# A hybrid decoder step on one core: shift rows moved ahead in the sync queue, past forget rows loaded early, pass-one units two to a tile, sample keys turned in pairs

## What is computed

```
h = x @ w_in                                   # columns for four head groups
A  y_a = u * (w_s @ LN(v) + b_s)               # u, v = gelu of two column ranges
B  s = q k^T/8 + c[q] - c[k]; p = softmax(s); y_b = p v      # "fox": c = cumsum(log forget)
C  gates * (compressed, selected, window attention)          # "nsa": one kv head per branch
   k_cmp = gelu(blocks of 32 rows @ w1) @ w2
D  y_d = d_b * conv3(d_c * d_h)
   samples: the same with keys and values taken from paged caches
x = LN(alpha*x + concat(y_a..y_d) @ w_out);  x = LN(alpha*x + MoE(x))
out: y, new k/v rows, log forget rows, window state, conv state (last 2 rows of d_c*d_h), v of A
```

## Time and profile before

| | us |
|---|---|
| median of 3 runs | 1379.12 (1375.01 to 1380.24) |
| the profiled execution | 1370.15 |
| its span, first to last instruction | 1368.4 |
| PE busy | 1162.9 (85%) |
| DVE busy | 419.5 (31%) |
| ACT busy | 316.4 (23%) |
| mean granted clock of PE, of full speed | 0.898 |

### The profile page before, as it was taken

The page is one execution under the profiler, slowest core; times in us unless marked ns, Lnnn a source line. Parts: engine busy times, 40 slices in busy tenths (PEclk is TensorE's granted clock), DMA queues, the critical chain, the costliest instruction groups (busy, mean ns, idle before and its releaser), DMA issues.

```text
span 1368.4 us, 13724 instructions
## 1 busy us (share of the span) xinstructions
PE 1162.9 (85%) x4624; PEld 609.5 (45%) x4625; DVE 419.5 (31%) x908; ACT 316.4 (23%) x628; POOL 82.3 (6%) x124
## 2 busy tenths in 40 slices
PE   7999998899999864998679989999389999999800
PEld 6647654344545321335444534555244444444400
DVE  2112433354435311114232312324611111111158
ACT  0102334452211531432211101111011111111133
POOL 3100000000000010000000000000011101011062
PEclk9999999999998886997659999998589999999965
DMA  7201103101000920300600614112258776957373
GB/s 224 80 20 54 62 0 122 28 2 45 1 1 2 21 46 19 108 1 0 184 1 9 240 62 154 62 62 78 92 177 293 279 248 231 321 193 277 143 290 132
DMA packets 105034, 149.23 MB, mean 109 GB/s; under 512 B 23482, under 2 KB 78074, under 8 KB 104954
## 3 DMA queue, kind: packets, MB, share of 16 engines
q1 hardware_dynamic: 88250, 112.63, 27.8%
q0 software_dynamic: 6464, 22.56, 4.7%
q10 hardware_dynamic: 10272, 13.40, 2.7%
HBM read 118.50 MB, written 32.02 MB: 110 GB/s over the span
## 4 chain that ended last, share of the span: by engine, by line
PE 77%; DVE 9%; SPq 5%; DMA 4%; issue 3%; ACT 2%; POOL 0%; POOLq 0%; DVEq 0%; ACTq 0%
PE psum_all L1305 17%; PE psum_all L1863 12%; PE psum_all L1783 9%; PE psum_all L1421 7%; PE psum_all L1851 6%; PE psum_all L1376 4%; PE psum_all L1451 3%; DMA arena<-in_w_exp_down 3%; PE psum_all L1485 2%; SPq L799 2%; PE psum_all L1834 1%; PE psum_all L1517 1%; PE psum_all L1538 1%; PE psum_all L1693 1%; PE psum_all L1600 1%
## 5 line engine op out<-in xcount | busy, mean ns | idle before, releaser
L1305 PE MATMUL psum_all<-arena 128*128 128x512 f32 (+7 forms) x800 | 236.8, 468 | 0.0
L1863 PE MATMUL psum_all<-arena 128*128 x400 | 181.8, 609 | 11.9 <-DMA arena<-in_w_exp_down 9.7
L1305 PEld LDWEIGHTS psum_all<-arena 128*128 128x128 f32 (+1 forms) x800 | 131.3, 183 | 91.4 <-issue 65.7
L1863 PEld LDWEIGHTS psum_all<-arena 128*128 128x128 f32 x400 | 76.1, 195 | 100.4 <-issue 100.4
L1783 PE MATMUL psum_all<-arena 128*128 128x512 f32 (+1 forms) x288 | 118.4, 593 | 0.0
L1421 PE MATMUL psum_all<-arena 128*128 128x512 f32 (+1 forms) x288 | 102.1, 510 | 0.9 <-ACT arena L1066 0.9
L1027 ACT ACTIVATE psum_all<-psum_all,neg_max 128x128 f32<-128x128 f32 (+7 forms) x96 | 65.6, 684 | 142.4 <-DVE neg_max L1995 142.2
L1851 PE MATMUL psum_all<-arena 128*128 x200 | 90.1, 593 | 0.9 <-ACT arena L1249 0.9
L1783 PEld LDWEIGHTS psum_all<-arena 128*128 128x128 f32 (+1 forms) x288 | 50.2, 184 | 61.6 <-issue 61.6
L1376 PE MATMUL psum_all<-arena 64*128 64x512 f32 (+3 forms) x288 | 63.2, 520 | 12.0 <-ACT psum_all L1027 12.0
L1421 PEld LDWEIGHTS psum_all<-arena 128*128 128x128 f32 x288 | 48.5, 198 | 51.4 <-issue 51.2
(11 more groups left out here) (388 smaller groups left out, 1252.0 us busy)
## 6 DMA issues: line engine op xcount, KB each, us to landing
arena<-in_w_exp_gate SPq DMA_DIRECT2D x16, 1024.0 KB, 8.3
arena<-in_w_exp_up SPq DMA_DIRECT2D x16, 1024.0 KB, 10.8
arena<-in_w_exp_down SPq DMA_DIRECT2D x16, 1024.0 KB, 12.8
slot_rows<-arena ACTq DMA_DIRECT2D x25, 512.0 KB, 6.8
arena<-in_x_prompt SPq DMA_DIRECT2D x16, 512.0 KB, 3.6
arena<-in_cache_fox_kv SPq DMA_DIRECT2D x32, 256.0 KB, 2.9
arena<-in_w_in SPq DMA_DIRECT2D x2, 2048.0 KB, 9.2
arena<-in_cache_nsa_kv SPq DMA_DIRECT2D x32, 128.0 KB, 2.1
```

Source lines behind the costliest of these rows:

```text
L1305: ins = nc.tensor.matmul(row_bank(j)[p0:p0 + n, 0:cn], xT[:, k, tok0(t):tok0(t) + n], wv[:, k, c0:c0 + cn], start=(k == 0), stop=(k == KD ...
L1863: ins = nc.tensor.matmul(psum[0][:], xT_slot[:, k, :], arena[:, bass.ds(w_at + k * 2 * F, 2 * F)], start=(k == 0), stop=(k == KD - 1))
```

## The change

Four parts. (1) SP: the page table and the 32 forget row loads go to the start of G_CQ. The conv_s stores, with a semaphore apart from conv_p's, go behind the nsa shift rows; those who reuse z_p's space wait for conv_p alone. (2) Pass one: two units are put behind the last tile of G_CKV, and G_A's tiles get 2, 2, 2, 2, 2, 2, 2, 1, 1 instead of 3, 3, 3, 3, 2, 2, 1, 1, 0; the logs of the fox sums move a tile ahead, the gate activations to tile 8 of G_A. (3) PE's wait for all exps of pass one moves from work unit 0 to 2. (4) Sample stage: fox units go by head pair outside and sequence inside, keys are turned and scored in pairs, and P times V goes by page outside and sequence inside.

```diff
@@ -312,7 +312,7 @@
             if br != "cmp":
-                units += [(u, b, pr) for b in range(4) for pr in range(2 if br == "fox" else 1)]
+                units += [(u, b, pr) for pr in range(2 if br == "fox" else 1) for b in range(4)]
         SW = PAST + NS
@@ -357,6 +357,7 @@
         conv_stored = sem("conv_stored")
+        conv_p_stored = sem("conv_p_stored")
         s_masks = sem("s_masks")
@@ -551,7 +552,8 @@
         STATS_AFTER.update({G_CKV * TILES + t: 1 for t in range(NT)})
-        STATS_AFTER.update({G_A * TILES + t: n for t, n in enumerate((3, 3, 3, 3, 2, 2, 1, 1, 0))})
+        STATS_AFTER.update({G_CKV * TILES + NT: 2})
+        STATS_AFTER.update({G_A * TILES + t: n for t, n in enumerate((2, 2, 2, 2, 2, 2, 2, 1, 1))})
         STATS_AFTER.update({N_ROWJ + i: int(i % 3 < 2 or i >= 14) for i in range(18)})
@@ -612,7 +614,8 @@
             sp.wait_ge(out_sem, 16 * outs_n[0])
-            sp.wait_ge(conv_stored, 16 * 2 * (1 + NB))
+            sp.wait_ge(conv_stored, 16 * 2 * NB)
+            sp.wait_ge(conv_p_stored, 16 * 2)
@@ -723,13 +726,25 @@
-            def store_slow(dst, src):
-                sp.dma_start(dst, src, allow_slow_non_contiguous=True).then_inc(conv_stored, 16)
+            def store_slow(dst, src, done):
+                sp.dma_start(dst, src, allow_slow_non_contiguous=True).then_inc(done, 16)
+            def load_pages(cache, dst, n, first, done):
+                with sp.Fori(0, n // NPG) as i:
+                    table = [sp.value_load(pages[0:1, bass.ds(i * NPG + (first + k), 1)], min_val=0, max_val=NPOOL - 1)
+                             for k in range(NPG)]
+                    for k, page in enumerate(table):
+                        sp.dma_start(dst[:, bass.ds(i * NPG + k, 1), :], cache[bass.ds(page, 1)]).then_inc(done, 16)
...
                     load_w(g + 1)
+                if g == G_CQ:
+                    sp.dma_start(pages[:], page_table.rearrange("(o b) n -> o (b n)", o=1)).then_inc(pages_loaded, 16)
+                    sp.wait_ge(pages_loaded, 16)
+                    load_pages(cache_fox_logf[0].rearrange("n p h -> n p h"), lf_past, NB * NPG, 0, lf_past_in)
                 for t in range(TILES):
@@ -778,34 +793,24 @@
                 fs = slice(f * P, f * P + P)
-                store_slow(conv_p[0, 0, :, fs].rearrange("j p -> p j"), z_p[:, f, SEQ:SEQ + 2])
-                for b in range(NB):
-                    store_slow(conv_s[0, b, :, fs].rearrange("j p -> p j"), z_s[:, f, b, TN:TN + 2])
...
-            sp.dma_start(pages[:], page_table.rearrange("(o b) n -> o (b n)", o=1)).then_inc(pages_loaded, 16)
-            sp.wait_ge(z_used, 12)
+                store_slow(conv_p[0, 0, :, fs].rearrange("j p -> p j"), z_p[:, f, SEQ:SEQ + 2], conv_p_stored)
             for c in range(2):
...
                 sp.dma_start(cmp_w2[:, c, :], nsa_cmp_w2[0, c]).then_inc(cmp_w_in, 16)
-            sp.wait_ge(pages_loaded, 16)
-            load_pages(cache_fox_logf[0].rearrange("n p h -> n p h"), lf_past, NB * NPG, 0, lf_past_in)
             sp.wait_ge(rows_cleared, 1)
...
                                  sh_split[H * NT * b:H * NT * (b + 1), r, :]).then_inc(sh_rows, 16)
+            for f in range(2):
+                fs = slice(f * P, f * P + P)
+                for b in range(NB):
+                    store_slow(conv_s[0, b, :, fs].rearrange("j p -> p j"), z_s[:, f, b, TN:TN + 2], conv_stored)
             sp.wait_ge(y_done, N_FG)
@@ -957,7 +962,7 @@
             pool.wait_ge(z_used, 12)
-            pool.wait_ge(conv_stored, 16 * 2 * (1 + NB))
+            pool.wait_ge(conv_p_stored, 16 * 2)
             pool.memset(nsa_shift, 0.0).then_inc(rows_cleared, 1)
@@ -1087,8 +1092,9 @@
                         nc.scalar.activation(lf_e[:], lf_e[:], ACT.Ln, bias=lnc[:, 1:2]).then_inc(lf_parts, 1)
-                    if (g, t) == (G_A, 0):
+                    if (g, t) == (G_A, NT):
                         act.wait_ge(proj_copied, G_A * TILES)
+                        act.wait_ge(sh_ready, 1)
                         nc.scalar.activation(gates[:].rearrange("p t b h -> p t (b h)"), nsa_rows[:, :, 6 * DH:6 * DH + 12],
@@ -1098,7 +1104,7 @@
                         sum_exps(i)
-                    if (g, t) == (G_A, 0):
+                    if (g, t) == (G_CKV, NT):
                         log_sums(N_FOX, 0, H * NT)
@@ -1147,7 +1153,7 @@
             act.wait_ge(comp_done, 2)
-            act.wait_ge(conv_stored, 16 * 2 * (1 + NB))
+            act.wait_ge(conv_p_stored, 16 * 2)
             for c in range(2):
@@ -1406,7 +1412,7 @@
                         stat_scores(i)
-                    if (g, t) == (G_A, 3):
+                    if (g, t) == (G_A, 2):
                         turn_shifts(0, 0, H * NT)
@@ -1432,10 +1438,11 @@
                 elif u == 0:
-                    pe.wait_ge(st_summed, 2 * N_ST)
                     pe.wait_ge(z_used, 12)
...
                     pe.wait_ge(sh_rows, 16 * 6)
+                if u == 2:
+                    pe.wait_ge(st_summed, 2 * N_ST)
                 if u == N_FW:
@@ -1677,21 +1684,21 @@
                     nc.tensor.matmul(O, PTs[0:NS, NPG, :], v, start=True, stop=False, skip_group_check=True)
-                for b in range(4):
-                    Ob, bs_ = O[32 * b:32 * b + 32, :], 4 * g + b
-                    if br == "cmp":
-                        ins = nc.tensor.matmul(Ob, PTs[0:NC_S, 0, 32 * b:32 * b + 32], cmp_v_s[0:NC_S, bs_, :],
-                                               start=True, stop=True, tile_position=(0, 32 * b))
-                        continue
-                    for n in range(NPG):
+                if br == "cmp":
+                    for b in range(4):
+                        ins = nc.tensor.matmul(O[32 * b:32 * b + 32, :], PTs[0:NC_S, 0, 32 * b:32 * b + 32],
+                                               cmp_v_s[0:NC_S, 4 * g + b, :], start=True, stop=True, tile_position=(0, 32 * b))
+                for n in range(0 if br == "cmp" else NPG):
+                    for b in range(4):
+                        bs_ = 4 * g + b
                         if br == "fox":
...
                             v = win_cache[:, bs_, n, DH:2 * DH]
-                        ins = nc.tensor.matmul(Ob, PTs[:, n, 32 * b:32 * b + 32], v, start=False, stop=(n == NPG - 1),
-                                               skip_group_check=True, tile_position=(0, 32 * b))
+                        ins = nc.tensor.matmul(O[32 * b:32 * b + 32, :], PTs[:, n, 32 * b:32 * b + 32], v, start=False,
+                                               stop=(n == NPG - 1), skip_group_check=True, tile_position=(0, 32 * b))
                 ins.then_inc(so_ready, 1)
@@ -1703,13 +1710,16 @@
                     turn_keys(mine[0])
+                    turn_keys(mine[1])
                     new_scores(u)
...
                         turn_sample_p(u - 1)
-                    for i in mine:
-                        if i + 1 in mine:
-                            turn_keys(i + 1)
+                    for i in mine[::2]:
+                        if i + 2 in mine:
+                            turn_keys(i + 2)
+                            turn_keys(i + 3)
                         score_keys(i)
+                        score_keys(i + 1)
                     if br == "win":
@@ -2125,13 +2135,13 @@
                         split_forget()
-                    if (g, t) == (G_A, 0):
+                    if (g, t) == (G_A, NT):
                         make_gates()
...
                         row_max(i)
-                    if (g, t) == (G_A, 1):
+                    if (g, t) == (G_A, 0):
                         make_shifts(0, 0, H * NT)
-                    if (g, t) == (G_A, 3):
+                    if (g, t) == (G_A, 2):
                         split_shifts(0, H * NT)
@@ -2220,7 +2230,7 @@
             dve.wait_ge(lf_past_in, 16 * NB * NPG)
-            dve.wait_ge(conv_stored, 16 * 2 * (1 + NB))
+            dve.wait_ge(conv_p_stored, 16 * 2)
             for g in range(2):
...
                     for b in range(4):
```

More of the change, by code:

```diff
@@ L780, in _ @@
                 fs = slice(f * P, f * P + P)
-                store_slow(conv_p[0, 0, :, fs].rearrange("j p -> p j"), z_p[:, f, SEQ:SEQ + 2])
-                for b in range(NB):
-                    store_slow(conv_s[0, b, :, fs].rearrange("j p -> p j"), z_s[:, f, b, TN:TN + 2])
-            def load_pages(cache, dst, n, first, done):
-                with sp.Fori(0, n // NPG) as i:
-                    table = [sp.value_load(pages[0:1, bass.ds(i * NPG + (first + k), 1)], min_val=0, max_val=NPOOL - 1)
-                             for k in range(NPG)]
-                    for k, page in enumerate(table):
-                        sp.dma_start(dst[:, bass.ds(i * NPG + k, 1), :], cache[bass.ds(page, 1)]).then_inc(done, 16)
-            sp.dma_start(pages[:], page_table.rearrange("(o b) n -> o (b n)", o=1)).then_inc(pages_loaded, 16)
-            sp.wait_ge(z_used, 12)
```

(1 more changed line is left out.)

## The result

The changed kernel takes 1304.48 us (median of 4 runs, 1300.05 to 1314.16) against 1377.07 us for the kernel before on the same chip (4 runs, 1367.99 to 1380.24): ratio 0.949, 95% interval 0.942 to 0.956. Forecast were 1313.6 us, range 1300 to 1333. The profiled execution of the changed kernel took 1306.05 us with a span of 1304.3, so 64.1 us less than the 1368.4 of before, where the sum said 65.5. Measured a second time beside experiment 9 the changed kernel had a median of 1307.45 us and a span of 1307.8. Two profiles of one kernel thus differ by 3.5 us, and the four executions above have spans from 1298.3 to 1312.4. The expert part, from the last matmul of w_out to the last matmul of all, which nothing here touches, takes 354.8 to 361.7 us in the twelve profiles of this document.

What follows compares the result with a forecast made beforehand. The prediction took PE, 77% of the chain of waits, as the bound and looked where it stands still; 32.2 + 13.2 + 1.1 + 19 = 65.5 us against the earlier median of 1379.12 gave 1313.6 us, range 1300 to 1333.

Steps and rivals of the forecast that it cites:

- Shift rows, 32.2 us: First nsa scores: PE's 31.0 us DMA wait goes, plus 1.2 us for its clock; ends 25 and 33.5.
- Even 488.90 would do: SP's queue: arriving as late as 488.90, the shift rows would land near 495, ahead of PE at 500.75.
- Pass one, 13.2 us: G_A's tiles: spreading the stat units saves 9.7 + 3.9 + 0.9 − 1.3 us; ends 5 and 14.5.
- Rival B: Pass one: later gelu and gate work on ACT moves waits into D; term 5, time 1322 us, chance 0.10.
- The wait at u = 2, 1.1 us: Start of pass two: two units' scores fill the 4.01 us wait, first exp little earlier; ends 0 and 4.
- Sample stage, 19 us: Sample stage: key pairs 13.6 − 1 us plus P times V 6.5 us; ends −3 and 25.
- Late next: Second half of the fox pages: the change saves some 5.5 of 7.3 us before their reader, so they land in time.
- rival D: Sample stage: fox pages bound it, a few us more than reckoned are lost; about 1317 us, chance 0.02.
- A: Sample stage: pairs bring little, scores wait for copies or don't overlap; stage gives 5 us, time 1328, chance 0.15.
- C: Shift rows: SP held in an issue or rings slow, half of 32 us stays; time 1330 us, chance 0.06.
- E: Whole kernel: no change, something other than the DMA ends the 31.0 us wait; about 1379 us, chance 0.03.
- F: Behind 500 us: PE without rests gets a lower clock, kernel slower; 1397 us at 0.80, chance 0.02.

Runs made afterwards that it cites:

- experiment 9: The kernel of experiment 8 timed longer, in six executions, beside the changed kernel: median 1306.48 us, ratio 0.950.
- experiment 1: Changed kernel with the 16 conv_s stores back ahead and one wait for all 18 stores, forget rows still early: 1305.48 us, ratio 0.950.
- experiment 2: Changed kernel with the forget row loads back in front of the shift rows, conv_s stores still behind: 1321.20 us, ratio 0.962.
- experiment 3: Changed kernel with PE's wait for all exps of pass one back at work unit 0: 1308.90 us, ratio 0.949.
- experiment 5: Changed kernel with sample keys turned and scored one by one in the old unit order, P times V as changed: 1323.83 us, ratio 0.961.
- experiment 6: Changed kernel with P times V of the samples back to sequences outside and pages inside, pairs kept: 1311.14 us, ratio 0.954.
- experiment 8: Changed kernel with SP reading the first four page numbers of the second fox group before its wait for the buffer: 1303.63 us, ratio 0.947.

## Why the prediction was right, point by point

**Shift rows, 32.2 us: right in sum, its parts not needed.** The wait went and so did the slow restart (four records in 1.13 us, not 2.08). Between the first P times V and the nsa scores 28.5 us went, not 31.0: PE's same records are busy 41.3 us there, at a clock of 0.95, against 39.4 at 1.00, and a wait for ACT holds it 0.6. Up to the compress stage another 3.0 came. Together 31.5. The table and the 32 forget loads held SP from 113.86 to 161.86, not to 156, and cost PE nothing, as forecast. The clearing could start 9.5 us after the first store (436.01 to 445.52), not a ninth of 34 us; with all 18 stores ahead (experiment 1) it started at 472.00. That did not matter. The step "two conv_p stores stay ahead, the 16 conv_s stores go behind" was costed as harmless, and as part of what lets the rows go early; experiments 1 and 2 show that it adds nothing to the forget loads, though alone it would bring 21.5 of the 31.0 us. "Even 488.90 would do" was the right reading: experiment 1 is that case. The split was to end last; in fact SP itself came last (452.86), held by pe_rows.

**Pass one, 13.2 us: 14.1 at the first D matmul, and 13.5 there by undoing it.** The 9.7 us of idle, the tiles of 9.43 and 8.73 and the 0.9 us at D are gone, the new wait at unit 16 is 0.98 us (forecast 1.3), and unit 34 doesn't wait. Rival B, that it is given back, fell; only 1.35 us went in the D phase.

**The wait at u = 2, 1.1 us: 1.2 where it acts**, and by the nsa scores nothing that is shown (experiment 3). The mechanism was right: the scores of two units fill the wait, which falls from 4.0 us to 1.0, and then VectorE's shifts and ACT's exps hold PE for 1.3 and 1.6. From the end of the wait to the first P times V it takes 4.1 us, where it took 5.3.

**Sample stage, 19 us: 22.9, both terms too small.** The pairs were put at 13.6 − 1 = 12.6; the turns and scores take 16.6 us less than before (48.3 to 31.7), and 17.0 in experiment 5. The step that failed is "a pair should take 1.1 + 1.0 us ... I take 0.85 each": a pair takes 2.0, the full 1.1 less, and the copies make no wait. P times V was put at 6.5 and is 8.9 in its own rows: 2.7 in the first fox job, 3.6 in the last, and 0.74 in three of the four nsa jobs and 0.43 in the fourth, where 0.2 was taken. The reason is one: 32 records of 256 columns on four strips take 1.93 us, 8 turns of 0.24, so each turn costs about what one record does (0.22). The Trainium skill's 2.38 times for three column tiles (TensorE: Matmul & The Clock Gate, Part 3, Measured speedup vs the span model) had given 3.0 us as an estimate; here, with four strips of another width, it is 3.7 times against the 7.1 us in a row, which is an estimate itself, since no run has the records in a row.

The same page has matmuls start and end strictly in program order (The mechanism). The prediction read "no overlap" and 7.1 us out of that, which goes too far: the last record of one strip and the first of the next could still overlap. But the trace doesn't agree with the order either. Line L1693 of the kernel before in the first fox job, and its first four records alone (count; least, median and largest duration in ns; first and last start):

```profile
L1693 PE MATMUL psum_all<-arena x32: 379/379/404, 742.7 to 746.9; 128*32 128x256 f32 x32
...
L1693 PE MATMUL psum_all<-arena x4: 379/379/404, 742.7 to 743.4; 128*32 128x256 f32 x4
```

The first four records, all of one strip, start 0.22 us apart. With eight records to a strip and the strips one after the other, starts in program order would take at least 28 × 0.22 = 6.0 us from the first to the last; they take 4.2, in the old order of experiment 6 too (692.8 to 697.0). From the fifth record on they come in twos, so a strip seems to begin while the one before still has records to go. That the two of a pair belong to neighbouring strips is read from the spacing; the trace doesn't name the strip.

**Late next, "enough, barely": wrong.** The fox pages were to keep 1.8 us of slack. Instead PE waited 2.8 us for them at the key turns: one of the prediction's own signs of being wrong, and the mechanism of rival D, which had a chance of 0.02. From the issue of the first of these loads to the turn that reads them it was 28.7 us before (750.60 to 779.32); without the wait it would now be 19.7 (697.62 to 717.35), so the change saved 9.0 us there, not 5.5, and the pages landed 22.5 us behind the first issue, not the 21.4 reckoned. Together 4.6: the slack of 1.8 became a wait of 2.8. So D took place, yet the time was not D's, because what had eaten the slack was mostly a larger gain: in sum 16.6 + 8.9 − 2.8 = 22.7, against 22.9 measured.

**The total.** By terms 31.5 + 14.1 − 0.2 + 22.9 = 68.3; another 2.7 us were lost between the compress stage and the first key turn and 3.0 in w_out, with 1.5 regained later, hence 64.1 (64.2 by the last matmul). Rivals A, C, E and F fell: the pairs brought more than reckoned, no wait for the shift rows is left, and the mean clock is 0.903, where F needed 0.81. "All behind pass two ... shifts with it" was thus off by 4 us.

That 65.5 us were summed and 64.1 measured is in part luck. The sample stage gave 3.9 us more than its term and pass one 0.9, while the shift rows and the u = 2 term gave 1.8 less and other stretches, mostly at the lower clock, took 4.4 back. The base was luck too. Against the profiled execution the sum said 1304.6, and the medians came at 1304.5 and 1307.5; but that execution was 7 us below the median of its kernel (1377.07). By medians the change is 72.6 us, and 66.9 in the second measurement (1374.32 to 1307.45), and where the difference to 64.1 lies no profile here shows. The forecast itself, 1313.6, was 9 us too high.

## What to carry to other kernels

When two things are moved out of one queue's way, add up the queue for each move alone: a move whose successor has slack already buys nothing. Small matmuls on strips of 32 columns should take turns over the strips; in the innermost loop four of them cost about one here (128 rows, fp32, 64 and 256 columns of data). And a stage that gets shorter catches up with its own prefetch, so reckon its slack with the largest gain of the range, not with the likeliest.

## What the runs showed of the hardware that was not expected

Two fp32 score matmuls of 512 columns on neighbouring strips take 1.05 us, one takes 1.04, two on the same strip 1.91. Four strips that take turns overlap almost wholly (1.93 us for 32 records, where one strip after the other takes 4.59).

Where the clock falls moves with the kernel. The stretches at 1.2 GHz took 17.0 us of the D phase before and 20.6 after, with the same matmuls, and the phase 138.8 and 140.1 us. A faster stage can meet such a stretch: the turns and sums behind the fox pages take 2.3 us longer in the changed kernel than in experiment 6, whose P times V is slower, and they do so without the wait as well (experiment 8).

PE stands for 1.4 to 2.6 us in the fox pass with only "issue" named in experiments 3, 6 and 9, and not in the other nine profiles; experiments 9 and 8 are one kernel. It belongs to no edit.

The small load of pe_rows holds SP 9.39 and then 2.06 us in its two issues behind two stores, 8.47 and 1.89 in experiment 2, 9.49 and 7.95 behind all 18 in experiment 1, and 17.20 and 5.32 behind all 18 in the kernel before. So against experiment 1 fewer stores ahead shorten the second issue, not the first, and what makes the first 17.20 in one kernel with 18 stores ahead and 9.49 in another wasn't tried.
